# An RWKV-7 scan on one core: its triangular inverse with two products a level instead of three, and its w_ada tiles split high and low

## What is computed

```python
def _adaln(cond, w, b):
    return jax.nn.silu(cond) @ w + b            # cond: c_ctx and c, w: [1024, 6144]

def step(s, inp):                               # _wkv_scan, per token, batch and head
    r_t, w_t, k_t, v_t, kk_t, a_t = inp
    sa = jnp.einsum('bhvk,bhk->bhv', s, -kk_t)
    s = (s * w_t[:, :, None, :] + sa[..., :, None] * (kk_t * a_t)[..., None, :]
         + v_t[..., :, None] * k_t[..., None, :])
    return s, jnp.einsum('bhvk,bhk->bhv', s, r_t)

def _block(x, mod, s0, lp, ffn):
    shift1, scale1, gate1, shift2, scale2, gate2 = jnp.split(mod[:, None, :], N_MOD, axis=-1)
    m, s_fin = _mixer(x * (1 + scale1) + shift1, lp, s0)   # proj = h @ w_in, scan, Hyena, merge, w_o
    x = _layer_norm(DEEPNORM_ALPHA * x + gate1 * m, lp['ln_g'][0], lp['ln_b'][0])
    f = ffn(x * (1 + scale2) + shift2)                     # dense in layer 0, 8 experts in layer 1
    return _layer_norm(DEEPNORM_ALPHA * x + gate2 * f, lp['ln_g'][1], lp['ln_b'][1]), s_fin
```

## Time and profile before

| | us |
|---|---|
| median of 3 runs | 2327.38 |
| lowest, highest | 2324.06, 2327.42 |
| the profiled execution, own time | 2320.44 |
| its span from first to last instruction | 2318.7 |
| TensorE busy in it | 2056.6 (89%) |
| VectorE, ScalarE busy | 1124.6 (49%), 814.5 (35%) |
| scan of layer 0, of layer 1 | 148 to 527, 980 to 1318 |

### The profile page before, as it was taken

How to read it: one execution, slowest core, us unless ns; L and a number is a source line. 1 busy time by engine, 2 the same in 40 slices (tenths; PEclk the granted TensorE clock), 3 DMA queues, 4 the chain that set the end, 5 groups by cost and what they waited for, 6 DMA issues and landing times.

```text
span 2318.7 us, 31750 instructions
## 1 busy us (share of the span) xinstructions
PE 2056.6 (89%) x13589; PEld 1747.7 (75%) x13589; DVE 1124.6 (49%) x1441; ACT 814.5 (35%) x1029; POOL 107.4 (5%) x161
## 2 busy tenths in 40 slices
PE   6789999996779997889999967789999999999996
PEld 2766776665569986677777746688988989899895
DVE  0634533335565546544534356544545545454454
ACT  1333323333143433333343332333433334333332
POOL 3010100000020000011010000000000000000000
PEclk9868989998889998789998979799999999999998
DMA  8413324333045553212222412335555555555552
GB/s 276 134 32 108 103 66 128 105 98 128 15 147 182 183 194 114 86 37 92 92 93 92 129 55 73 109 110 193 182 182 168 174 191 166 187 167 180 179 166 82
DMA packets 247421, 301.32 MB, mean 130 GB/s; under 512 B 8428, under 2 KB 224081, under 8 KB 247153
## 3 DMA queue, kind: packets, MB, share of 16 engines
q1 hardware_dynamic: 240112, 286.28, 38.4%
q0 software_dynamic: 4192, 11.28, 1.5%
q10 hardware_dynamic: 2976, 1.73, 0.2%
HBM read 297.69 MB, written 1.57 MB: 129 GB/s over the span
## 4 chain that ended last, share of the span: by engine, by line
PE 46%; DVE 5%; ACT 2%; issue 1%; ACTq 0%; DVEq 0%
PE PS L654 8%; PE PS L655 8%; PE PS L656 8%; PE PS L973 4%; PE PS L975 4%; PE PS L974 4%; PE PS L688 2%; DVE WL L1364 1%; ACT WH L1084 1%; PE PS L822 1%; PE PS L808 1%; PE PS L762 1%; PE PS L828 1%; PE PS L846 1%; PE PS L841 0%
## 5 line engine op out<-in xcount | busy, mean ns | idle before, releaser
L654 PE MATMUL PS<-HTH,WH 128*128 128x256 f32 x2448 | 722.8, 295 | 63.9 <-issue 25.6
L1364 DVE TENSOR_TENSOR WL<-WRING,WH 128x2048 fp32r<-128x2048 f32 (+1 forms) x213 | 460.2, 2162 | 536.0 <-ACT WH L1084 534.1
L655 PE MATMUL PS<-HTL,WH 128*128 128x256 f32 x2448 | 704.8, 288 | 0.0
L656 PE MATMUL PS<-HTH,WL 128*128 128x256 f32 x2448 | 704.1, 288 | 0.0
L1084 ACT ACTIVATE WH<-WRING 128x2048 fp32r<-128x2048 f32 (+1 forms) x213 | 385.6, 1810 | 695.9 <-PE PS L656 448.6
L654 PEld LDWEIGHTS PS<-HTH,WH 128*128 128x128 f32 x2448 | 477.8, 195 | 81.5 <-issue 63.9
L655 PEld LDWEIGHTS PS<-HTL,WH 128*128 128x128 f32 x2448 | 477.8, 195 | 0.3
L656 PEld LDWEIGHTS PS<-HTH,WL 128*128 128x128 f32 x2448 | 476.3, 195 | 0.0
L688 PE MATMUL PS<-WRING,CONDT 128*2 128x256 f32 x768 | 198.4, 386 | 6.7 <-DMA WRING<-in_w_ada 5.6
L973 PE MATMUL PS<-WH,AH 128*128 128x512 f32 x440 | 171.9, 391 | 13.5 <-DVE WL L1364 13.5
L975 PE MATMUL PS<-WL,AH 128*128 128x512 f32 x440 | 171.3, 389 | 0.0
(11 more groups left out here) (327 smaller groups left out, 2386.5 us busy)
## 6 DMA issues: line engine op xcount, KB each, us to landing
WRING<-in_exp_w_in SPq DMA_DIRECT2D x80, 1024.0 KB, 5.5
WRING<-in_w_ada SPq DMA_DIRECT2D x48, 1024.0 KB, 5.3
WRING<-in_w_in SPq DMA_DIRECT2D x42, 1024.0 KB, 5.5
WRING<-in_exp_w_out SPq DMA_DIRECT2D x40, 1024.0 KB, 4.9
WRING<-in_ffn_w_in SPq DMA_DIRECT2D x22, 1024.0 KB, 5.2
WRING<-in_ffn_w_out SPq DMA_DIRECT2D x11, 1024.0 KB, 4.9
WRING<-in_w_o SPq DMA_DIRECT2D x8, 1024.0 KB, 4.9
WRING<-in_exp_w_in SPq DMA_DIRECT2D x16, 512.0 KB, 3.9
```

The costliest lines, as they stand in the source:

```text
L654: mm(out, h[:, kb, c], hi[:, kb, :], start=kb == 0, stop=False)
L655: mm(out, h[:, kb, c], lo[:, kb, :], start=False, stop=False)
L656: last = mm(out, s[:, kb, c], hi[:, kb, :], start=False, stop=kb == k - 1)
L1364: tt(WL[:, m % 2, 0:k * w], WRING[:, n % RING, 0:k * w], WH[:, m % 2, 0:k * w].bitcast(F32), ALU.subtract)\
```

## The change

The inverse's off-diagonal part F is kept (FM), starting as the matrix's own strict part, and with it the transpose of F in PSUM bank bk[1]. At each level VectorE masks the transpose into Y (two tiles YS in turn), and TensorE adds two products, F with Y to the transpose and Y with F to F. ScalarE copies F once a level; VectorE adds the identity at the end. A level is one step instead of two: a block has 18 steps, HALF is 10, and a layer has 144 slots. The fp32 transposes of step 3 are replaced by products with the identity in fp32r. The fill parts are as many as before and are spread over the fewer slots, with more than one to a slot where needed.

The w_ada tiles of the scans (all but the first 8 of layer 0) are now split like w_in tiles, and multiplied as two fp32r products for each of 8 blocks of rows: WH with CONDS (the conditions' high and low halves, 4 columns) and WL with the high half (2 columns). `col` adds the low half's row in a second operation. What the start of a tile needs and is not yet due is put right ahead of its first part (`needs`).

```diff
-FIRST_LEVEL, REFINE = 4, 4 + 1 + 2 * (LEVELS - 1)
+FIRST_LEVEL, REFINE = 4, 4 + LEVELS
...
-            if second[0] == "in":
-                after += [(2 + q, ("split", tile, q)) for q in range(4)]
+            after += [(2 + q, ("split", tile, q)) for q in range(4)]
             fill[-1] = (fill[-1][0], after)
+            needs["part" if second[0] == "in" else "ada", second[1], second[2]] = [item for delay, item in after]
...
-                if slot * len(fill) // slots > used:
+                while slot * len(fill) // slots > used:
                     piece, after = fill[used]
+                    if piece[3] == 0:
+
+                        early = [item for due, item in pending if item in needs.get(piece[:3], [])]
+                        sched += early
+                        pending = [entry for entry in pending if entry[1] not in early]
...
         def split(n):
-            return tiles[n][0] != "ada"
+            return not opening(tiles[n])
...
+                    if split(n):
+                        mm(PS[0:4, bank_of[n], 0:256], CONDS[:, kb, :], h[:, kb, :], start=kb == 0, stop=False,
+                           skip_group_check=True)
+                        last = mm(PS[0:2, bank_of[n], 0:256], CONDS[:, kb, 0:2], s[:, kb, :], start=False, stop=True,
+                                  skip_group_check=True)
...
+                    pe.wait_ge(ev(f"level{x}"), j * LEVELS + 1)
+                    for s in range(4):
+                        last = mm(four(bk[1], s), FM[x][:, s, :], IDR[:, :], start=s == 0, stop=False, skip_group_check=True)
+                    last.then_inc(ev(f"turned{x}"), 1)
+                    mm(PS[:, bk[0], :], IDR[:, :], FM[x][:, :, :], start=True, stop=False, skip_group_check=True)
                 elif step < REFINE:
...
+                    lv = step - FIRST_LEVEL
+                    y = YS[lv % 2][x]
+                    pe.wait_ge(ev(f"crossed{x}"), j * LEVELS + lv + 1)
+                    pe.wait_ge(ev(f"level{x}"), j * LEVELS + lv + 1)
+                    if lv < LEVELS - 1:
                         for s in range(4):
...
+                            last = mm(four(bk[1], s), FM[x][:, s, :], y[:, s, :], start=False, stop=True, skip_group_check=True)
+                        last.then_inc(ev(f"turned{x}"), 1)
...
                     for s in range(4):
...
+                        last = mm(four(bk[0], s), y[:, s, :], FM[x][:, s, :], start=False, stop=True, skip_group_check=True)
                     last.then_inc(ev(f"update{x}"), 1)
...
+                elif FIRST_LEVEL <= step < REFINE - 1:
+                    lv = step - FIRST_LEVEL
                     act.wait_ge(ev(f"update{x}"), j * LEVELS + lv + 1)
...
+                    fn(FM[x][:, :, :], four(bk[0]), ACT.Copy).then_inc(ev(f"level{x}"), 1)
...
+                def off_block(lv):
+
+                    dve.wait_ge(ev(f"turned{x}"), j * LEVELS + lv + 1)
+                    if lv >= 2:
+                        dve.wait_ge(ev(f"update{x}"), j * LEVELS + lv - 1)
+                    tt(YS[lv % 2][x][:, :, :], PS[:, bk[1], :].rearrange("p (a t) -> p a t", a=4),
+                       q4(LEVEL[:, 1 - d, lv, :]), ALU.mult).then_inc(ev(f"crossed{x}"), 1)
...
+                elif FIRST_LEVEL <= step < REFINE - 1:
+                    off_block(step - FIRST_LEVEL + 1)
+                elif step == REFINE - 1:
+                    dve.wait_ge(ev(f"update{x}"), (j + 1) * LEVELS)
+                    tt(FM[x][:, :, :], PS[:, bk[0], :].rearrange("p (a t) -> p a t", a=4), q4(IDENT[:, :]), ALU.add)\
+                        .then_inc(ev(f"inverse{x}"), 1)
```

More of the change, by code:

```diff
@@ L137, in schedule @@
         sched += [("values", l), ("in", l, 7), ("wprep", l), ("barrier",)]
-        order, fill, pieces = [], [], 8
+        order, fill, pieces, needs = [], [], 8, {}
         behind = [(l, j) for j in range(ADA_HEAD, ADA)] + [(l + 1, j) for j in range(ADA_HEAD) if l + 1 < LAYERS]
@@ L279, in build @@
         CONDT = sb("CONDT", [P, 16])
-        ADAR = sb("ADAR", [2, 2, 256])
+        CONDS = sb("CONDS", [P, KB, 4], F32R)
+        ADAR = sb("ADAR", [4, 2, 256])
         A2 = sb("A2", [P, DR])
@@ L329, in build @@
         MAT = lane(1024, "MAT", [P, 4, 4, T])
[L330 to L333, removed]
+        FM = lane(4096, "FM", [P, 4, T], F32R)
+        YS = [lane(3072, "YS0", [P, 4, T], F32R), lane(4608, "YS1", [P, 4, T], F32R)]
         EX = lane(3072, "EX", [P, G, T + 1])
@@ L390, in build, with opening @@
         number = {t: n for n, t in enumerate(tiles)}
+        def opening(tile):
+            return tile[0] == "ada" and tile[1] == 0 and tile[2] < ADA_HEAD
         split_no, k = [], 0
@@ L393, in build @@
             split_no.append(k)
-            k += t[0] != "ada"
+            k += not opening(t)
         ring_in = [sem(f"ring_in{i}") for i in range(RING)]
@@ L695, in turn @@
                 pe.wait_ge(ev("ada_row"), l * ADA + j + 1)
+                r = 4 if split(n) else 2
                 for b in range(2):
-                    last = pe.transpose(PS[:, bank_of[n], 256 + 2 * b:258 + 2 * b], ADAR[:, j % 2, b * P:(b + 1) * P],
-                                        IDENT[0:2, 0:2])
+                    last = pe.transpose(PS[:, bank_of[n], 256 + r * b:256 + r * b + r], ADAR[0:r, j % 2, b * P:(b + 1) * P],
+                                        IDENT[0:r, 0:r])
                 last.then_inc(ev("ada_turn"), 1)
@@ L801, in scan @@
                     last.then_inc(ev(f"rhs{x}"), 1)
-                elif step < REFINE:
-                    lv, second = (step - FIRST_LEVEL + 1) // 2, (step - FIRST_LEVEL) % 2 == 0
-                    if not second:
-                        pe.wait_ge(ev(f"level{x}"), j * LEVELS + lv)
-                        for s in range(4):
[L808 to L820, removed]
+                    pe.wait_ge(ev(f"level{x}"), j * LEVELS + 1)
@@ L840, in scan @@
                         for s in range(4):
-                            last = mm(half(bk[1], s), GM[x][:, s, :], src[x][:, s, :], start=True, stop=True)
+                            last = mm(half(bk[1], s), FM[x][:, s, :], src[x][:, s, :], start=True, stop=True)
                         last.then_inc(ev(f"solve{x}"), 1)
@@ L1111, in cond @@
                 act.sem_inc(ev("cond_silu"), 1)
+                fn(CONDS[:, :, 0:2], CONDT[:, :].rearrange("p (g k) -> p k g", g=G), ACT.Copy).then_inc(ev("cond_hi"), 1)
             def row(l, j):
@@ L1122, in line @@
                     act.wait_ge(ev("ada_turn"), l * ADA + j - 1)
-                fn(ADAR[:, j % 2, :], PS[0:2, bank_of[n], 0:256], ACT.Copy).then_inc(ev("ada_row"), 1)
+                r = 4 if split(n) else 2
+                fn(ADAR[0:r, j % 2, :], PS[0:r, bank_of[n], 0:256], ACT.Copy).then_inc(ev("ada_row"), 1)
             def mod_columns(l, w):
@@ L1375, in bias @@
             def bias():
+                dve.wait_ge(ev("cond_hi"), 1)
+                steps(tt(CONDS[:, :, 2:4], CONDT[:, :].rearrange("p (g k) -> p k g", g=G), CONDS[:, :, 0:2].bitcast(F32),
+                         ALU.subtract))
                 dve.wait_ge(ev("start_ps"), 2)
@@ L1414, in col @@
                     steps.wait()
-                tt(MODT[:, l, c, :], PS[:, bank_of[n], 256:260].rearrange("p (b c) -> p b c", c=2), bias, ALU.add)\
-                    .then_inc(dve_read, 1)
+                if split(n):
+                    turned = PS[:, bank_of[n], 256:264].rearrange("p (b c) -> p b c", c=4)
+                    steps(tt(MODT[:, l, c, :], turned[:, :, 0:2], bias, ALU.add))
+                    steps.wait()
+                    tt(MODT[:, l, c, :], MODT[:, l, c, :], turned[:, :, 2:4], ALU.add).then_inc(dve_read, 1)
+                else:
+                    tt(MODT[:, l, c, :], PS[:, bank_of[n], 256:260].rearrange("p (b c) -> p b c", c=2), bias, ALU.add)\
+                        .then_inc(dve_read, 1)
                 steps.wait_for(dve_read, read_no[n])
```

44 lines of the change are left out of this document (11 added, 33 removed).

## The result

The changed kernel takes 2350.1 us (median of four executions, 2349.1 to 2355.8) against 2325.7 before: the ratio is 1.0114, with an interval of 1.0091 to 1.0137. It is slower by 24 us where 23 were forecast, for about 2350 us, on the side that had 0.59. The execution whose trace follows is the slowest of the four, 2355.8 us, 35 above the profiled execution before; the other three lie between 2349.1 and 2350.2.

A forecast was written before the change was run, and what follows sets the result against it. TensorE's own work was taken to bound the scans; 512 us of work, 143 idle and 85 lost to the clock make 740 instead of 717, plus 2 outside: 2345, about 2350 us as median. Forecast's range 2325 to 2380, 8 in 10: 2270 to 2410.

The forecast's parts named there:

- Work removed: TensorE in both scans: cheaper w_ada parts and fewer level products save 67 and 53 us, 120 in all (bounds 52 and 134).
- The term for w_ada: w_ada parts in the scans: 0.53 us each instead of 0.96, saving 41 us in layer 0 and 27 in layer 1.
- Tile starts: First parts of tiles wait for quarters of their own split at 23 and 15 starts: 61 us in layer 0, 29 in layer 1.
- Step 0: Level 6 of the other lane waits for a VectorE mask queued behind a lane's step 0, in 14 blocks: 25 us.
- Idle time in all: TensorE's idle time in the two scans after the change: 143 us, against 50 before (bounds 50 and 170).
- Clock: Loss to 1.2 GHz in the scans, 0.6 us per us idle: 85 us against 35 before; mean clock about 0.86.
- (1): Rival: the waits come in the scans but the clock doesn't follow; scans 690 us, 2302 us in all; chance 0.15.
- (2): Rival: waits of half the length and 10 us for step 0; idle 95 us, 2276 us in all; chance 0.15.
- (3): Rival: the scans stay bound by TensorE's work, 597 us; 2209 us in all; chance 0.04.
- (4): Rival: scan waits at the upper bound, 170 us, and 1.2 GHz held between them, 115 us; 2409 us; chance 0.21 with its twin.
- its twin: w_ada products get no cheaper, 0.96 us a part, 68 us on top of the forecast: 2418 us; chance 0.21 with (4).
- The size of the threshold: Growth of the scans' idle time at which the change's net effect is nought: 77 us, where 93 was forecast.

The follow-up runs named there:

- inverse_alone: The changed kernel with w_ada left unsplit, keeping the new inverse with 18 steps: 2318.7 us, 0.23% below the kernel before.
- early: The changed kernel with a split's four quarters put 1, 1, 2 and 2 slots behind the end of the tile before, not 2 to 5: 2307.0 us.
- filler: The changed kernel with 14 products, their results overwritten, ahead of the wait for the split at 38 tile starts: time falls by 44 us.
- both_padded: The run both with two more unused products of 248 columns beside each pair of the w_ada tiles: 2240.0 us.
- both: The changed kernel with quarters 1, 1, 2, 2 and row, turn, column 1, 2, 3 slots behind a tile's end, VectorE's step 0 behind its next slot's operation: 2232.3 us.
- step0_later: The changed kernel with VectorE doing step 0's five operations behind its operation of the next slot: 14 us faster by the medians, 10 by the ratios.
- split_bank: The kernel before with w_ada split, quarters 1, 1, 2, 2 and row, turn, column 1, 2, 3 slots behind a tile's end: 91 us idle; time not stated.

## Why the prediction was right, point by point

**The bound.** The reading that TensorE's work sets the time of the scans held for the kernel before; after the change it no longer does, as forecast.

**Work removed: 120 forecast, 132 measured** (634 to 502). The inverse saved 50 us, where 52 were forecast (inverse_alone). The term for w_ada was a little small: a part takes 0.47 us, not 0.53. Eight single-pass products of two parts in a row start 0.12 apart:

```profile
544.55 0.28 PE L700 MATMUL PS<-WH,CONDS 128*4 128x256 f32 x1
544.67 0.28 PE L702 MATMUL PS<-WL,CONDS 128*2 128x256 f32 x1
544.79 0.28 PE L700 MATMUL PS<-WH,CONDS 128*4 128x256 f32 x1
```

**Tile starts: 61 and 29 us forecast, 64.5 and 32.9 measured**, in exactly the 23 and 15 places. The cause was named by half: the quarter ended last, and the column, due in the same slot, only 0.6 us before it. `early` showed it, by 42 us that stayed. The forecast of the time didn't depend on this, a cure did.

**Step 0: 25 us forecast, 23.2 measured** at L830. But its removal is worth 10 to 14 us alone and 25 with the rest, so 38 for idle time and clock together was too much.

**Idle time in all: 143 forecast, 142 measured.** Here two errors cancel: tile starts and step 0 took 121 us and not 115, all other causes 21 and not 28.

**Clock: 85 us forecast, 111 measured.** This is the mis-sized term. I took 0.6 us per us of idle time, below the 0.7 of before, on the argument that close waits share a slow stretch. It was 0.78, and the mean clock 0.79 and 0.81 instead of 0.86. The 0.7 itself was read wrongly: of the 88 us at 1.2 GHz in the scans before, 27 belong to two stretches that had begun ahead of the scans, and no wait in them caused these (columns as in the earlier trace rows).

```profile
127.00:148.00 21.00, 18.85 (x56) 11.64 (x56) 9.69 (x7) 6.17 (x10) 3.84 (x4) 0.51 0.17 50
148.00:161.60 13.60, 8.59 (x31) 5.78 (x32) 4.67 (x9) 2.43 (x5) 3.61 (x5) 0.50 0.00 1
963.00:981.00 18.00, 17.33 (x56) 11.02 (x54) 7.91 (x3) 5.28 (x9) 3.84 (x4) 0.52 0.10 36
981.00:994.50 13.50, 8.54 (x30) 5.71 (x31) 4.61 (x9) 2.42 (x4) 3.62 (x5) 0.50 0.00 1
```

In the changed kernel only layer 1's scan begins so, with 13 us. Leaving these out, a microsecond of idle time cost 0.50 us before (24.5 for 49) and 0.75 after (107 for 142). So the price didn't fall when the waits came closer together, it rose by half.

Why it rose isn't settled. Left out in the same way, it is 0.27 to 0.70 in the kernels with w_ada unsplit and 0.72 to 0.89 in those with it split, filler (0.43) and both_padded (0.67) apart, and in four pairs that differ in the split alone it goes from 0.50 to 0.89, 0.27 to 0.80, 0.40 to 0.87 and 0.35 to 0.85. That speaks for the four-pass products, which the split takes away, having held the clock up; so does both_padded (0.67), with more work in their place, against both (0.85). But in the pair nearest to the change, inverse_alone and the changed kernel, it is 0.70 and 0.75: without any split it was already far above 0.50. And the price goes with the amount of idle time just as well: 0.27 to 0.50 in the four other unsplit kernels, with 24 to 49 us idle, and 0.70 to 0.89 in all that have 70 or more, but for filler.

The Trainium skill (TensorE: Matmul & The Clock Gate, "A second HAM failure mode: psum-queue depth-cycling") says that short idle times between groups of products make the clock swing between its levels; the trace agrees, with 33 stretches at 1.2 GHz in the two scans where before there were 11.

**Outside: 2 us forecast, 5 us less measured** (1604 to 1599).

**The sum.** 740 was forecast for the scans and 755 measured in this execution: 10 us too much work and 26 too little for the clock. Outside, 7 us less came than forecast, and the scans before were cut 2 us wider in the prediction, so this execution is 10 above the 2345 of its sum. The prediction then added 7 us, as the median before was 7 above its profiled execution; after, the median is 6 below it. That the median is met to 1 us is luck: errors of 6 to 26 us cancel. The direction and the size of the wait terms are not luck.

**The rivals.** (1), waits without the clock, fell with the clock of 0.79 and 0.81. (2) and (3) fell with the count and length of the waits. Of (4) the clock's half all but came, 111 of 115 us, and the idle time didn't (142, not 170); its twin, w_ada parts at 0.96 us, fell with the 0.47. The size of the threshold (77 us more idle time) is borne out too: of kernels with the same products, early has 68 us more than before and is 0.7% faster, step0_later has 86 and is 0.7% slower, the changed kernel has 93 and is 1.1% slower.

**What stays open.** How much of the dearer clock is the lack of dense products, how much the amount of idle time and how much the way the waits are spread isn't told apart. And the 91 us of idle time in split_bank weren't followed slot by slot.

## What to carry to other kernels

When an engine that is the bound is relieved, read next to its busy time what each of its steps waits for and which items stand ahead of that in the other engines' lists; a start that was just in time becomes a wait. If two things release it and both were put at the same distance, moving one leaves the wait to the other: 27.8 of 29.7 us stayed at the w_in starts of layer 0. And work taken from TensorE is worth its time only as long as nothing else sets the pace of the steps it fills: here the split of w_ada, some 80 us less work, cost 18 to 31 us, while the placing of two lines of the schedule and the new inverse, without that split, saved 87.

## What the hardware showed that I hadn't expected

Adding products made the kernel faster: 62 us of empty work in filler bought 44 us. It covered 38 us of idle time, less than it cost, so the gain came through the clock, which was at 1.2 GHz for 116 us and not 307. 66 us of it in both_padded cost 8 us. And a scan at 0.99 of the full clock with 307 us of busy TensorE takes as long as one at 0.92 with 278.
